# A pad and a moved table: the on-chip tensors of a split-fp32 transformer kernel shifted by 96 and 224 bytes

## The chip, the core and the metric

The kernel runs on one core of a Trainium2 chip. The metric is the device time of one execution in microseconds; before the change it is 969.88 us, the median of 3 runs (968.15 to 973.4).

## What is computed

Two transformer blocks, one after the other, on 256 tokens of width 1024, all in float32. The first mixes a windowed attention (8 heads, 2 key heads, with a sink logit) and a bidirectional chunkwise mLSTM, whose states come from 256 context tokens; its shifts, scales and gates come from a conditioning vector through `w_ada`. The second prepends 16 meta tokens (272 in all) and has two SwiGLU layers around a windowed attention with a gated linear attention. What fills the time are the dense products:

```
x = x + gt_m * rms_norm(concat(att, mlstm) @ w_out, g)
x = x + gt_f * rms_norm((silu(h @ Wg) * (h @ Wu)) @ w_ffn_out, g)            # width 2816
h = h + 0.5 * (silu(n @ ffn1_w_gate) * (n @ ffn1_w_up)) @ ffn1_w_down        # 272 tokens
h = h + (sigmoid(ga) * (ya @ w_branch_att) + sigmoid(gb) * (yb @ w_branch_gla)) @ w_out
out = rms_norm(h + 0.5 * swiglu(rms_norm(h), ffn2...), final)[:, 16:]        # 256 tokens
```

## The kernel before

**Layout of the work.** Activations lie transposed: 128 partitions by 8 tiles `k` of the model width, and the tokens (256, 258 or 272 columns) along the free dimension. A weight panel of 128 x 128 is the stationary operand, a token tile the moving one, and a product is written to a PSUM bank (`acc` or `wk`) of 512 columns.

**Split products.** Each float32 product is made of three fp32r products: the weights and the activations are each split into a rounded high part and the rest, and `split_mm` (L2003 to L2007) adds high x high (L2005), low activation x high weight (L2006) and high activation x low weight (L2007). L2398 (`mixed_part`), L2134 (`two_groups`) and L2203 to L2205 (`by_token`, where the weights are the moving operand) do the same in other orders.

**The rings.** Weights stream from HBM by SP's DMA queue into `raw`, four slots of 1408 floats per partition. For each slot ScalarE rounds `raw` to `hi` (L621), VectorE writes `lo = raw - hi` (L1143), and TensorE takes 24 matmuls from a slot of 1024 floats or 33 from one of 1408. ScalarE's split of slot j waits for TensorE's use of the slot's former content (`mm_done`), VectorE's for `hi_ready`, TensorE for `lo_ready`.

**The stages**, by the time of the profile: the first block's input projections with mLSTM and attention between them (to 190 us), `gu0` (gate and up of the first SwiGLU, 258 columns: the 256 tokens and two more, 190 to 320), `dn0` (its down product, 256 columns, 320 to 385), `gu1` and `dn1` (272 columns, 385 to 525 and 525 to 590), the second block's projections, attention and linear attention (590 to 740), `wout2` and `gu2` (256 columns, 740 to 890) and `dn2` (to the end). `n_high` and `n_low` hold the activations of `gu0`, `gu1` and the second mixer, `mixH` and `mixL` those of the output products and of `gu2`, `g_high` and `g_low` those of the down products, `n5H` and `n5L` the 512 tokens of the first projections.

**Where tensors lie.** `sbuf` (L117) takes on-chip tensors one behind the other from a stack; each begins at the next multiple of 32 bytes in the partition, and scopes that are closed give their space to later ones. The first one, `cst`, begins at byte 16512, a multiple of 64, and is 1544 bytes long, so what follows is shifted. Worked out from the declarations, the start of each in bytes, modulo 64 and 256:

| tensor | start | mod 64 | mod 256 |
|---|---|---|---|
| `cst` (identity, ones) | 16512 | 0 | 128 |
| `raw` | 33184 | 32 | 160 |
| `hi` / `lo` | 55712 / 78240 | 32 | 160 |
| `mixH` / `mixL` | 100960 / 109152 | 32 | 96 |
| `n5H` / `n5L` | 144928 / 161312 | 32 | 32 |
| `n_high` / `n_low` | 121888 / 132128 | 32 | 32 |
| `g_high` / `g_low` | 168032 / 192096 | 32 | 96 |
| `sg` | 216032 | 32 | 224 |
| `hbuf`, `row3` | 218240, 220416 | 0 | 128, 0 |
| `Sm` (first attention) | 183840 | 32 | 32 |
| `kdT`, `kS2`, `av2`, `gvtok`, `kdtok`, `St`, `attm`, `bias2`, `Sm2`, `pT2` | 192704 to 221440 | 0 | |

The steps inside a tensor are multiples of 64 bytes in all operands of the dense products: 128 weight columns are 512 bytes, a tile of 256 columns 1024, one of 272 columns 1088, the tiles of `mH` 1280 bytes apart, and the frames begin 16 columns (64 bytes) into a row. So all of these operands begin at 32 modulo 64.

Of the kernel before, what the change touches and what calls it, by code (L numbers as in the profile page):

```python
# [14 lines left out]
P = 128  # L15
# [99 lines left out]
def program(nc, dr, out):  # L115
    with ExitStack() as root:
        def sbuf(stack, name, shape, dt=F32):  # L117
            return stack.enter_context(nc.sbuf_tensor(name, shape, dt))
# [2 lines left out]
            return root.enter_context(nc.semaphore(name))  # L121


        cst = sbuf(root, "cst", [P, 3 * P + 2])
        ident, ones, swap, pick = cst[:, 0:P], cst[:, P:2 * P], cst[:, 2 * P:3 * P], cst[:, 3 * P:3 * P + 2]
        vec = sbuf(root, "vec", [P, NV])
# [4 lines left out]
        crow = sbuf(root, "crow", [P, D])  # L131
        R = sbuf(root, "R", [P, KD, TM])
        raw = sbuf(root, "raw", [P, RING, SLOT])
        slabs1 = ExitStack()
        slab_hi = sbuf(slabs1, "slab_hi", [P, RING, SLOT])
        slabs1.close()
        hi = sbuf(root, "hi", [P, RING, SLOT], F32R)
        lo = sbuf(root, "lo", [P, RING, SLOT], F32R)
        sinkn = sbuf(root, "sinkn", [P, 16])
        negm = sbuf(root, "negm", [P, 32])  # L140
        staged = ExitStack()
        stage = sbuf(staged, "stage", [P, 4, 1024])
        staged.close()
# [2655 lines left out]
```

## Time and profile before

| | |
|---|---|
| median of 3 runs | 969.88 us |
| span of the profiled execution | 969.3 us |
| TensorE busy | 954.7 us, 7543 matmuls |
| VectorE / ScalarE busy | 640.4 / 494.7 us |
| GpSimd busy | 68.8 us |
| read from HBM | 174.32 MB, 181 GB/s over the span |

The span runs from the first instruction to the last of one profiled execution. TensorE's matmuls overlap: a matmul's record lasts about 0.28 us while the next one begins after some 0.12 us, so the busy time does not tell how fast they run; what tells is the distance from one start to the next, or the number of matmuls in a stretch.

### The profile page before, as it was taken

Reading aid. Unit: us, or ns where it says so; the run is one execution under the profiler, and the core shown is the slowest. Engines: PE = TensorE matmul, PEld = TensorE weight load, DVE = VectorE, ACT = ScalarE, POOL = GpSimd, SP = SyncE. Lnnn points to the kernel's source line nnn. Section 1 sums busy time; section 2 is a strip of 40 time slices with the busy share of each in tenths; the row PEclk is TensorE's granted clock in tenths of the full one; section 3 lists DMA queues with packets and bytes.
Section 4 is the critical chain, followed back from the end, with each engine's and each line's share of the span. In section 5 each row is a group of like instructions: output and inputs, shape, how many; then the busy total and the mean of one; then the engine's idle time right before and its main releaser. Section 6 shows DMA issues by size and latency. Waiting matters only on the chain.

```text
span 969.3 us, 19405 instructions
## 1 busy us (share of the span) xinstructions
PE 954.7 (98%) x7543; PEld 886.8 (91%) x7543; DVE 640.4 (66%) x990; ACT 494.7 (51%) x762; POOL 68.8 (7%) x100
## 2 busy tenths in 40 slices
PE   8999999999999999999999999999999999999997
PEld 3776778899999999899999999999989999999997
DVE  4788887687666774765555546665778666565654
ACT  3755547664454543554444434645565555444540
POOL 0012002200000021000000000200210100000000
PEclk9999999999999999999999999999999999999999
DMA  9982437546566795276665944663445567567841
GB/s 348 384 282 89 131 131 237 181 165 201 180 187 184 203 299 164 63 215 174 173 174 169 238 114 137 212 185 88 132 134 173 167 181 209 179 182 220 215 119 43
DMA packets 189184, 176.06 MB, mean 182 GB/s; under 512 B 7313, under 2 KB 177825, under 8 KB 188753
## 3 DMA queue, kind: packets, MB, share of 16 engines
q1 hardware_dynamic: 183456, 154.29, 53.7%
q0 software_dynamic: 4960, 17.64, 5.2%
q10 hardware_dynamic: 720, 3.49, 0.9%
q8 instruction: 31, 0.51, 0.2%
q14 instruction: 17, 0.13, 0.1%
HBM read 174.32 MB, written 1.05 MB: 181 GB/s over the span
## 4 chain that ended last, share of the span: by engine, by line
PE 88%; DVE 6%; DMA 2%; ACT 2%; issue 1%; SPq 1%; POOL 0%; DVEq 0%; ACTq 0%
PE acc L2005 24%; PE acc L2006 24%; PE acc L2007 24%; PE acc L2398 2%; DMA slab_hi<-in_w_ada 1%; DMA stage<-in_w_late 1%; PE acc L2203 1%; PE acc L2205 1%; PE acc L2204 1%; PE wk L2005 1%; DVE lo L1143 1%; PE wk L2007 1%; PE wk L2006 1%; PE wk L2702 1%; PE wk L2134 1%
## 5 line engine op out<-in xcount | busy, mean ns | idle before, releaser
L1143 DVE TENSOR_TENSOR lo<-raw,hi 128x1024 fp32r<-128x1024 f32 (+1 forms) x259 | 331.6, 1291 | 211.4 <-ACT hi L621 211.1
L621 ACT ACTIVATE hi<-raw 128x1024 fp32r<-128x1024 f32 (+1 forms) x260 | 283.6, 1099 | 133.7 <-PE acc L2007 123.5
L2005 PE MATMUL acc<-n_high,hi 128*128 128x272 f32 (+3 forms) x1016 | 290.8, 286 | 0.3 <-DVE hbuf L1671 0.3
L2006 PE MATMUL acc<-n_low,hi 128*128 128x272 f32 (+3 forms) x1016 | 289.4, 285 | 0.0
L2007 PE MATMUL acc<-n_high,lo 128*128 128x272 f32 (+3 forms) x1016 | 288.4, 284 | 0.0
L2005 PEld LDWEIGHTS acc<-n_high,hi 128*128 128x128 f32 (+1 forms) x1016 | 191.6, 189 | 2.7 <-issue 1.4
L2006 PEld LDWEIGHTS acc<-n_low,hi 128*128 128x128 f32 (+1 forms) x1016 | 191.1, 188 | 0.5
L2007 PEld LDWEIGHTS acc<-n_high,lo 128*128 128x128 f32 (+1 forms) x1016 | 191.0, 188 | 0.2
L2006 PE MATMUL acc<-g_low,hi 128*128 128x256 f32 (+1 forms) x528 | 149.1, 282 | 0.0
L2005 PE MATMUL acc<-g_high,hi 128*128 128x256 f32 (+1 forms) x528 | 148.9, 282 | 0.0
L2007 PE MATMUL acc<-g_high,lo 128*128 128x256 f32 (+1 forms) x528 | 148.7, 282 | 0.0
L2005 PE MATMUL acc<-mixH,hi 128*128 128x256 f32 x400 | 113.0, 282 | 0.5 <-DVE gab L1844 0.4
L2006 PE MATMUL acc<-mixL,hi 128*128 128x256 f32 x400 | 112.3, 281 | 0.0
L2007 PE MATMUL acc<-mixH,lo 128*128 128x256 f32 x400 | 112.3, 281 | 0.0
L2006 PEld LDWEIGHTS acc<-g_low,hi 128*128 128x128 f32 x528 | 99.8, 189 | 0.0
L2005 PEld LDWEIGHTS acc<-g_high,hi 128*128 128x128 f32 x528 | 99.2, 188 | 0.2 <-issue 0.2
L2007 PEld LDWEIGHTS acc<-g_high,lo 128*128 128x128 f32 x528 | 99.2, 188 | 0.0
L2006 PEld LDWEIGHTS acc<-mixL,hi 128*128 128x128 f32 x400 | 76.6, 192 | 0.0
L2005 PEld LDWEIGHTS acc<-mixH,hi 128*128 128x128 f32 x400 | 75.1, 188 | 1.4 <-DVE gab L1844 0.7
L2007 PEld LDWEIGHTS acc<-mixH,lo 128*128 128x128 f32 x400 | 75.1, 188 | 0.0
L566 POOL TENSOR_TENSOR sq<-sq 128x256 f32<-128x256 f32 (+1 forms) x28 | 25.6, 915 | 479.9 <-ACT sq L923 431.9
L923 ACT ACTIVATE sq<-R (+3 forms) x36 | 15.9, 440 | 57.6 <-DVE R L1715 49.9
(424 smaller groups left out, 1246.6 us busy)
## 6 DMA issues: line engine op xcount, KB each, us to landing
raw<-in_w_in SPq DMA_DIRECT2D x52, 512.0 KB, 4.1
raw<-in_w_ffn_in SPq DMA_DIRECT2D x44, 512.0 KB, 3.8
raw<-in_ffn_w_gate SPq DMA_DIRECT2D x44, 512.0 KB, 3.9
raw<-in_ffn_w_up SPq DMA_DIRECT2D x44, 512.0 KB, 3.8
raw<-in_ffn_w_down SPq DMA_DIRECT2D x32, 704.0 KB, 4.8
stage<-in_w_late POOLq DMA_DIRECT2D x24, 512.0 KB, 5.1
raw<-in_w_ffn_out SPq DMA_DIRECT2D x16, 704.0 KB, 6.2
raw<-in_w_out SPq DMA_DIRECT2D x16, 512.0 KB, 4.4
```

The costliest lines, as they stand in the source:

```text
L566: ins = pool.tensor_tensor(sq[:, 0, 0:width], sq[:, 0, 0:width], sq[:, k, 0:width], ALU.add)
L621: act.activation(hi[:, j, 0:width], raw[:, j, 0:width], ACT.Copy).then_inc(hi_ready, 1)
L923: act.activation(sq[:, k, 0:width], R[:, k, t0:t0 + width], ACT.Square).then_inc(sq_ready, 1)
L1143: dve.tensor_tensor(lo[:, j, 0:width], raw[:, j, 0:width], hi[:, j, 0:width].bitcast(F32), ALU.subtract).then_inc(lo_ready, 1)
L2005: pe.matmul(out_, wH, xH, start=start, stop=False)
L2006: pe.matmul(out_, wH, xL, start=False, stop=False)
L2007: return pe.matmul(out_, wL, xH, start=False, stop=stop)
L2134: ins = pe.matmul(bank[:, T * m:T * m + T], ws[:, j, w], xs[:, k, 0:T], start=k == 0 and m == 0 and n == 0, stop=k == KD - 1 and n == 2, s ...
L2203: pe.matmul(out_, n5H[:, k, rows], hi[:, k // 2, w], start=k == 0, stop=False)
L2204: pe.matmul(out_, n5H[:, k, rows], lo[:, k // 2, w], start=False, stop=False)
L2205: return pe.matmul(out_, n5L[:, k, rows], hi[:, k // 2, w], start=False, stop=k == KD - 1)
L2398: ins = pe.matmul(out_, ws[:, j, w], xs[:, k, :], start=k == 0 and m == 0 and n == 0, stop=k == KD - 1 and n == 2, skip_group_check=True)
```

## The change

A tensor of 24 floats (96 bytes) that nothing uses is declared ahead of `cst`, and `negm`, a table of 32 floats (128 bytes), is declared between `raw` and `slab_hi`/`hi` in place of behind `sinkn`. No instruction, no wait and no order is changed.

```diff
+        sbuf(root, "pad_0", [P, 24])
         cst = sbuf(root, "cst", [P, 3 * P + 2])
...
         raw = sbuf(root, "raw", [P, RING, SLOT])
+        negm = sbuf(root, "negm", [P, 32])
         slabs1 = ExitStack()
...
         sinkn = sbuf(root, "sinkn", [P, 16])
-        negm = sbuf(root, "negm", [P, 32])
```

By the same working, everything moves by 96 bytes, and what lies between `raw` and `sinkn` (`slab_hi`, `hi`, `lo`, `sinkn`) by 224:

| tensor | start after | mod 64 | mod 256 |
|---|---|---|---|
| `cst` | 16608 | 32 | 224 |
| `raw` | 33280 | 0 | 0 |
| `hi` / `lo` | 55936 / 78464 | 0 | 128 |
| `mixH` / `mixL` | 101056 / 109248 | 0 | 192 |
| `n5H` / `n5L` | 145024 / 161408 | 0 | 128 |
| `n_high` / `n_low` | 121984 / 132224 | 0 | 128 |
| `g_high` / `g_low` | 168128 / 192192 | 0 | 192 |
| `sg` | 216128 | 0 | 64 |
| `hbuf`, `row3` | 218336, 220512 | 32 | 224, 96 |
| `kdT` to `pT2` | 192800 to 221536 | 32 | |

The last tensor ends at byte 229312.

## Rows read from the trace of the kernel before

**Rows 1.** The page: TensorE's share, its granted clock by slice, the chain that ended last

```profile
PE 954.7 (98%) x7543; PEld 886.8 (91%) x7543; DVE 640.4 (66%) x990; ACT 494.7 (51%) x762; POOL 68.8 (7%) x100
...
PEclk9999999999999999999999999999999999999999
...
PE 88%; DVE 6%; DMA 2%; ACT 2%; issue 1%; SPq 1%; POOL 0%; DVEq 0%; ACTq 0%
```

**Rows 2.** Busy time by stretch: us, each engine with its instructions, clock, DMA, GB/s

```profile
20.00:60.00 40.00, 38.20 (x240) 29.60 (x240) 32.76 (x71) 25.91 (x46) 3.91 (x10) 1.00 0.96 345
...
340.00:370.00 30.00, 30.00 (x267) 30.00 (x267) 21.36 (x22) 13.24 (x16) 8.00 (x8) 1.00 0.99 280
470.00:500.00 30.00, 30.00 (x242) 30.00 (x241) 17.67 (x19) 13.62 (x18) 0.00 (x0) 1.00 0.59 173
250.00:280.00 30.00, 30.00 (x251) 30.00 (x250) 19.36 (x28) 15.85 (x23) 0.00 (x0) 1.00 0.58 177
790.00:820.00 30.00, 30.00 (x258) 30.00 (x256) 19.64 (x21) 16.30 (x22) 0.00 (x0) 1.00 0.71 210
```

**Rows 3.** TensorE in order of time, 735 us: start us, duration us, instruction

```profile
734.98 0.28 PE L2005 MATMUL acc<-mixH,hi 128*128 128x256 f32 x1
...
735.89 0.28 PE L2007 MATMUL acc<-mixH,lo 128*128 128x256 f32 x1
```

**Rows 4.** The same view at 738 us, behind a piece of attention

```profile
736.77 1.02 PE L2702 MATMUL wk<-pT,av 16*64 16x128 f32 x12
...
738.21 0.28 PE L2007 MATMUL acc<-mixH,lo 128*128 128x256 f32 x1
...
738.92 0.28 PE L2007 MATMUL acc<-mixH,lo 128*128 128x256 f32 x1
```

**Rows 5.** Groups by shape: line, engine, instruction, shapes, count, busy us, mean ns, idle

```profile
L2006 PE MATMUL acc<-n_low,hi 128*128 128x272 f32 x400 | 115.7, 289 | 0.0
...
L2006 PE MATMUL acc<-mixL,hi 128*128 128x256 f32 x400 | 112.3, 281 | 0.0
...
L2006 PE MATMUL acc<-g_low,hi 128*128 128x256 f32 x352 | 98.0, 279 | 0.0
L2006 PE MATMUL acc<-n_low,hi 128*128 128x258 f32 x336 | 95.8, 285 | 0.0
...
L2006 PE MATMUL acc<-n_low,hi 128*128 128x256 f32 x272 | 75.6, 278 | 0.0
...
L2006 PE MATMUL acc<-g_low,hi 128*128 128x272 f32 x176 | 51.0, 290 | 0.0
```

**Rows 6.** TensorE in order of time: 512 columns, weights of 16 columns

```profile
68.41 0.40 PE L2006 MATMUL wk<-n5L,hi 128*16 128x512 f32 x1
...
69.33 0.40 PE L2007 MATMUL wk<-n5H,lo 128*16 128x512 f32 x1
```

**Rows 7.** The same: 512 columns, weights of 128 columns

```profile
109.60 0.39 PE L2204 MATMUL acc<-lo,n5H 128*128 128x512 f32 x1
...
110.52 0.40 PE L2205 MATMUL acc<-hi,n5L 128*128 128x512 f32 x1
```

**Rows 8.** The same: four plain fp32 matmuls of 256 columns, merged

```profile
63.37 1.02 PE L2183 MATMUL wk<-qT,c 128*128 128x256 f32 x4
```

**Rows 9.** Groups by shape: one operation on tensors at 0 and at 32 modulo 64

```profile
L1691 DVE TENSOR_TENSOR hbuf<-acc,inv 128x512 f32<-128x512 f32 x11 | 7.5, 681 | 0.0
...
L944 ACT ACTIVATE sg<-sg 128x512 f32<-128x512 f32 x11 | 7.0, 632 | 21.0 <-DVE sg L1663 21.0
...
L1685 DVE TENSOR_TENSOR sg<-acc,inv 128x512 f32<-128x512 f32 x10 | 6.8, 681 | 0.0
...
L948 ACT ACTIVATE g_high<-hbuf 128x512 f32 x9 | 5.7, 632 | 18.2 <-DVE hbuf L1671 18.2
```

**Rows 10.** Who waited for whom: us in total, times, longest

```profile
DVE lo L1143 <- ACT hi L621: 211.1, 178, 3.9
...
ACT hi L621 <- PE acc L2007: 123.5, 84, 4.2
```

## The prediction

> **What bounds the kernel now.** [...] Then the busy times by stretch: from about 190 us on, TensorE has work in every microsecond of a stretch, while VectorE is busy 15 to 21 us of 30 and the DMA engines move 173 to 280 GB/s [rows 2]. Last the waits: ScalarE's splits wait for TensorE to free a slot, VectorE's for ScalarE, so the ring is full and the matmuls set the pace [rows 10]. The time is the number of matmuls times the distance between their starts, and the change can only act on that distance, on the other engines' durations, or on the DMAs.
>
> [...] A stretch of 30 us sees every matmul whose record (0.28 us) touches it, so the distance is 30.28 us over the count [rows 2]: 113 ns in `dn0` (256 columns, 267 matmuls), 117 ns in `gu2` (256 columns, 258), 121 ns in `gu0` (258 columns, 251), 125 ns in `gu1` (272 columns, 242). [...] Single starts give the same with more digits: (735.89 - 734.98) / 8 = 114 ns in one streak of 256 columns [rows 3], (738.92 - 738.21) / 6 = 118 ns in the next one, behind twelve small attention matmuls [rows 4]. So there are two paces with the same tensors at the same addresses, the fast and the slow one. DMA traffic doesn't choose: the fast pace holds at a DMA share of 0.99, the slow one at 0.71 [rows 2].
>
> [...]
>
> **The change part by part.** No instruction is added, removed or moved, so each queue, SP's and GpSimd's too, issues the same in the same order; the pad and the moved table cost nothing by themselves.
>
> VectorE and ScalarE: `hbuf` begins at 0 and `sg` at 32 modulo 64, and the same operation takes 681 ns on either, ScalarE's 632 ns reading either [rows 9]. Nothing, in both directions.
>
> Dense matmuls, counts from the groups, each standing for three lines [rows 5]: 272 columns (400 + 176) x 3 = 1728; 258 columns 336 x 3 = 1008; 256 columns (400 + 352 + 272) x 3 = 3072. With those on other lines or banks I take 1780, 1060 and 3450. Some 1250 of the 256-column ones run at the fast pace (`dn0`, `w_out`, most of the second projections), 2150 at the slow one (all of `gu2` and `dn2`, part of the first projections). [...]
> - 256 columns, slow: 2150 x 6.7 = 14.4 us.
> - 256 columns, fast: the floor seems to be the columns plus about 2 ns, so 113.3 - 109 = 4.2 ns, x 1250 = 5.3 us.
> - 272 columns: 1780 x 6.7 = 11.9 us.
> [...]
> - 512 columns: some 290 x 6.7 = 2.0 us.
>
> The sum is 33.6 us. What hides it: before 190 us part of the matmuls wait beside attention, mLSTM and the start-up loads, so I let 95% through, 32 us. In the dense stages the next bound is far: 30 us of `dn0` hold 21.4 us of VectorE, of `gu2` 19.6 us, and a TensorE 4 to 6% faster keeps below that [rows 2]. `dn0` is the one place where the DMA engines are at 0.99 [rows 2]; should they bind there, some 3 us of the gain stay out.
>
> [...]
>
> DMAs: the rows written to `raw` begin at 0 instead of 160 modulo 256. Where that could count is the start-up, 20 to 60 us at a DMA share of 0.96 and 345 GB/s [rows 2], but the later stages have spare bandwidth. No row prices it; between -3 and +1 us, and I take 0.
>
> The small operands go the other way: `cst` and the second block's attention tensors leave 0 modulo 64 for 32. [...]
>
> [...]
>
> **The rivals.**
> [...]
> (b) Slower: the two paces are a pattern between the reads of weights and moving operand, started by what ran before [rows 3, 4]. The change moves `hi` and `lo` by 128 bytes against everything else modulo 256. If that is what chooses the pattern, the slow pace takes the fast stretches, 1250 x 4.4 = 5.5 us, 272 columns go from 125 to about 130 ns (1780 x 5 = 8.9 us) and 258 from 121 to 126 (5.3 us): 20 us, 990 us. [...] For: the slow pace exists. Against: modulo 128 the distance is kept.
> [...]
> [...]
>
> **How the numbers follow.** The profiled span of 969.3 us stands 0.6 us below the median of the runs, so the sum is made against 969.9: 969.9 - 32 = 938 us. Chances: forecast (930 to 947) 0.41; (c) 0.12; (d) 0.09; (a) 0.18; (b) 0.20. Faster by over 0.5% (under 965 us) is 0.62, within 0.5% (about what a measurement of this kernel can tell from no change) 0.18, slower 0.20. The range must keep (a) and half of (b) and most of (d): 918 to 982. The likeliest case alone would be 928 to 948.
>
> **What would show it.** Counts in 30 us of a steady stretch: `gu2` from 258 to about 273, `gu1` from 242 to about 255, `gu0` unchanged at 251. [...] If `dn0` falls to 258, (b). VectorE's and ScalarE's means must stay at 681 and 632 ns. The prediction is wrong if the path doesn't care for 64 bytes, which nothing in this trace can exclude.

## The result, and the profile after

The changed kernel takes 973.38 us (median, 971.48 to 975.48), the kernel before, run beside it, 970.01 us (968.03 to 973.4): a ratio of 1.0038, 95% interval 1.0023 to 1.0053. The forecast was 938 us. It is 0.4% slower, not 3% faster; no part of the expected gain came. The measured time lies in the range of 918 to 982 us only because the range was stretched to hold the rivals.

The page after has nearly the same TensorE time as [rows 1], 955.3 us against 954.7, and 9 in every slice of the clock, as before. The profiled execution is the quickest of the eight of the changed kernel (971.48 us).

```profile
span 969.7 us, 19405 instructions
...
PE 955.3 (99%) x7543; PEld 888.5 (92%) x7543; DVE 639.9 (66%) x990; ACT 494.6 (51%) x762; POOL 68.2 (7%) x100
...
PEclk9999999999999999999999999999999999999999
...
PE 88%; DVE 6%; ACT 2%; issue 1%; DMA 1%; SPq 1%; DVEq 0%; ACTq 0%
```

Busy time by stretch of the kernel after, columns and stretches as in [rows 2], and one stretch more, in `dn2`, where the kernel before has 257 matmuls, too:

```profile
20.00:60.00 40.00, 38.81 (x246) 30.46 (x246) 33.68 (x74) 26.46 (x47) 4.39 (x11) 1.00 0.95 352
...
340.00:370.00 30.00, 30.00 (x267) 30.00 (x266) 20.86 (x21) 13.23 (x16) 7.79 (x6) 1.00 0.91 281
470.00:500.00 30.00, 30.00 (x242) 30.00 (x242) 17.67 (x20) 13.62 (x18) 0.00 (x0) 1.00 0.60 170
250.00:280.00 30.00, 30.00 (x251) 30.00 (x250) 20.11 (x28) 15.15 (x22) 0.00 (x0) 1.00 0.59 176
790.00:820.00 30.00, 30.00 (x257) 30.00 (x256) 19.46 (x20) 16.52 (x22) 0.00 (x0) 1.00 0.69 210
905.00:935.00 30.00, 30.00 (x257) 30.00 (x256) 15.96 (x16) 12.10 (x12) 2.23 (x3) 1.00 0.80 234
```

From 190 us on each count is that of before to within one matmul: 267 in `dn0` (256 columns), 242 in `gu1` (272), 251 in `gu0` (258), 257 for 258 in `gu2` (256). Had the forecast's 6.7 ns a matmul come, `gu1` would show 255 and `gu2` 273. The other engines didn't move either: the operations of [rows 9] in the kernel after, groups by shape, the same columns, are 681 and 632 ns again.

```profile
L1692 DVE TENSOR_TENSOR hbuf<-acc,inv 128x512 f32<-128x512 f32 x11 | 7.5, 681 | 0.0
...
L945 ACT ACTIVATE sg<-sg 128x512 f32<-128x512 f32 x11 | 7.0, 632 | 21.1 <-DVE sg L1664 21.1
```

To see where 0.4% went I took the distances between starts stage by stage, leaving out gaps over 150 ns. Two stages of 256 columns show it: `w_out` (192 matmuls) goes from 114.3 to 117.8 ns, the second block's projections (816) from 115.2 to 116.8. `dn0` stays at 113.5, `gu2` and `dn2` at 117.7. Windows in which TensorE alone is listed (us, busy, count, clock, DMA share, GB/s), before:

```profile
163.00:178.00 15.00, 14.99 (x128) 1.00 0.70 219
...
690.00:720.00 30.00, 30.00 (x265) 1.00 0.44 135
```

and after:

```profile
163.00:178.00 15.00, 15.00 (x124) 1.00 0.62 206
...
690.00:720.00 30.00, 30.00 (x261) 1.00 0.44 134
```

`w_out` falls from 128 to 124 in 15 us, 3%. In all, 1247 of the 3456 starts of 256 columns were at most 116 ns apart before, 709 after: 538 x 4.5 ns = 2.4 us more. Some 264 matmuls of 512 columns became 3 ns shorter, 0.8 us less. That makes 1.6 us, for a difference of 3.4 us between the medians and 0.4 us between the two profiled spans (969.7 and 969.3). Part of the rest is a gain that works the other way: the start-up became quicker. TensorE has 246 matmuls from 20 to 60 us where it had 240, and reaches its 600th matmul at 111.2 us instead of 112.5.

### The profile page after: what moved, and what is told of

Same layout as the page of the kernel before. It is cut to its first block, busy times and chain, and to the rows that moved or that the text cites. A ratio compares the mean times of both kernels' runs of the same rounds, so it can differ in the third digit from the quotient of the medians.

```text
span 969.7 us, 19405 instructions
## 1 busy us (share of the span) xinstructions
PE 955.3 (99%) x7543; PEld 888.5 (92%) x7543; DVE 639.9 (66%) x990; ACT 494.6 (51%) x762; POOL 68.2 (7%) x100
## 4 chain that ended last, share of the span: by engine, by line
PE 88%; DVE 6%; ACT 2%; issue 1%; DMA 1%; SPq 1%; DVEq 0%; ACTq 0%
PE acc L2006 24%; PE acc L2007 24%; PE acc L2008 24%; PE acc L2399 2%; DMA slab_hi<-in_w_ada 1%; PE acc L2204 1%; PE acc L2206 1%; PE acc L2205 1%; PE acc L2135 1%; PE wk L2006 1%; PE wk L2008 1%; PE wk L2007 1%; DVE lo L1144 1%; PE wk L2703 1%; PE wk L2135 1%
```

## The experiments

Two questions: does the start modulo 64 matter at all, and what chooses between the two paces? The change does two things that can be made one at a time: the pad moves the operands of the dense products to multiples of 64 and keeps all distances; the table `negm` ahead of `hi` moves `slab_hi`, `hi`, `lo` and `sinkn` by 128 bytes against all other tensors, and so the weights against the moving operands. In what follows, distance means the start of the weights less the start of the moving operand, modulo 512 bytes. The steps between the weights used in `hi` and `lo` are multiples of 512 (but for the few products with 16 columns of weights), and so are those between the tiles of `mixH` and of `g_high` at 256 columns. The distance is 320 there in the kernel before and 448 in the kernel after. The tiles of `mH`, from which the 256-column frames of the second block's projections are read, are 1280 bytes apart: there the distance alternates between this value and one 256 bytes away, 64 and 320 before, 192 and 448 after.

The kernels of one group of experiments ran on one chip, beside the kernel before, and each is compared with the median of before on that chip.

**The pad alone** (`e_pad`):

```diff
+        sbuf(root, "pad_0", [P, 24])
         cst = sbuf(root, "cst", [P, 3 * P + 2])
```

> The pad of 96 bytes alone: everything moves by 96 bytes, the distance of hi and lo from the others is that of before. Theory A (addresses don't matter to the matmuls; the pace of 256 columns, 113.3 or 117.8 ns, is picked anew wherever TensorE starts again from a wait): between 968 and 975 us, with the stretches at 117.8 ns distributed anew, no rule in it. Theory C (the distance of the weights from the moving operands modulo 256 picks the pace): 970.0 us, the stretches of w_out and of the second projections at 113.3 ns as before.

967.62 us for 968.99, ratio 0.9985 (0.9974 to 0.9996). All big operands begin at 0 modulo 64, and `gu1` stays at 242, `gu0` at 251, `gu2` at 257. Nothing of the forecast's 6.7 ns a matmul is there. The time is just under what either theory said.

```profile
250.00:280.00 30.00, 30.00 (x251) 30.00 (x250) 20.11 (x28) 15.16 (x22) 0.00 (x0) 1.00 0.60 182
340.00:370.00 30.00, 30.00 (x257) 30.00 (x256) 19.73 (x20) 12.94 (x16) 7.41 (x6) 1.00 0.84 264
470.00:500.00 30.00, 30.00 (x242) 30.00 (x242) 17.58 (x18) 13.69 (x19) 0.00 (x0) 1.00 0.60 175
```

In this execution `dn0` runs at the slow pace (257) with the distance it had before. It is the slowest of the kernel's 11 executions (971.78 us, 4.2 above their median), so what it shows need not be what the others did. The start-up is quicker here, too: the 600th matmul begins at 111.1 us, in the kernel after at 111.2 and in its repetition at 111.3, against 111.8 to 112.5 in the nine profiled executions without the pad of 96 bytes. That is 1.2 us between the medians, most of the 1.37 us by which this kernel is faster than before.

**The table alone** (`e_negm`), starts staying at 32 modulo 64:

```diff
+        negm = sbuf(root, "negm", [P, 32])
         slabs1 = ExitStack()
         ...
         sinkn = sbuf(root, "sinkn", [P, 16])
-        negm = sbuf(root, "negm", [P, 32])
```

> The moved table alone: hi, lo and slab_hi move by 128 bytes, everything else stays, all at 32 modulo 64. Theory A: between 968 and 975 us, no rule in which stretches run at 117.8 ns. Theory C: 973.4 us as after the whole change, with w_out and the second projections at 117.8 ns.

973.95 us for 968.99, 1.0054 (1.0039 to 1.0069). It is at least the whole cost of the change: the moved table is what makes the kernel slower, the pad is not. The two parts add up: 4.96 us more and 1.37 us less are 3.6 us, and the whole change costs 3.4. The forecast of the distance theory was 973.4 us with `w_out` and the second projections at 117.8 ns, and they run at 117.7 and 117.6.

Its profiled execution holds something else: the granted clock falls to half (0.50) for 6.8 us in the first block. The stretch around it, in which TensorE alone is listed (us, busy, count, clock, DMA share, GB/s), and then the same in the kernel before:

```profile
155.70:162.50 6.80, 6.80 (x31) 0.50 0.98 357
```

```profile
155.70:162.50 6.80, 6.47 (x50) 1.00 0.94 336
```

From the 700th matmul to the 1100th the kernel before takes 54.0 us and this one 56.8, so the fall costs it 2.8 us. In the 5 us ahead of it TensorE did about the same in both (36 matmuls in 150 to 155 us before, 39 here), so these rows don't tell why it came. The profiled executions of `e_d0` and `e_all128` have a fall of 3.4 us at about the same place.

**A pad of 64 bytes** (`e_pad64`), which keeps starts modulo 64 and distances, as a control:

```diff
+        sbuf(root, "pad_0", [P, 16])
         cst = sbuf(root, "cst", [P, 3 * P + 2])
```

> A pad of 64 bytes, table in its old place: every tensor keeps its place modulo 64 and its distance from the others. Theory A: 968 to 975 us. [...]

The distance theory has 970.0 us here, too, with the same stretches at 113.3 ns as before. It took 968.23 us for 968.99, 1.0005 (0.9993 to 1.0016): nothing. Yet `dn2` runs at the fast pace in its profiled execution and at the slow one in that of the kernel before, with the same distances and starts modulo 64.

**A kernel of matmuls only** (`m1`) runs sections of 48 matmuls from tensors that are complete beforehand, each with other starts of the moving operand (`mo`) and the weights (`wo`). It computes nothing of the reference. Its loop, cut, where `term` goes through the three split products and `k` counts from 0 to 7:

```python
W = (wa, wa, wb)[term]; X = (xa, xb, xa)[term]
w = slice(wo + P * (k % 7), wo + P * (k % 7) + P)
x = slice(mo + 512 * (k % 7), mo + 512 * (k % 7) + width)
...
ins = pe.matmul(o, W[:, w], X[:, x], start=True, stop=True)
```

In theory A, the surplus is what a matmul takes beyond its columns' own time, and a full-rate stream is one of fp32r matmuls.

> A kernel of its own that computes nothing of the reference: sections of 48 fp32r matmuls on an otherwise idle core, with the operands of the three split terms in turn, moving and stationary operands begun 0, 4, 8, 16, 32, 48 bytes behind a multiple of 64, widths of 192 to 512 columns, and variants (same operands throughout, one high part, one weight, four banks, 16 weight columns, plain fp32). Theory A (the surplus belongs to the full-rate stream, whatever the start): 256 columns at 113 or 118 ns from every start, 272 at 125, 512 at 227 to 232, plain fp32 at 213 to 216 ns. [...]

TensorE in order of time in `m1` (start us, duration us, instruction). Each pair of lines is 20 starts apart; the sections stand in the order both at 0; moving operand 32 bytes on; weights 64 bytes on; both 32 bytes on:

```profile
22.27 0.28 PE L110 MATMUL acc<-xa,wb 128*128 128x256 f32 x1
...
24.67 0.28 PE L110 MATMUL acc<-xb,wa 128*128 128x256 f32 x1
...
47.42 0.28 PE L110 MATMUL acc<-xa,wa 128*128 128x256 f32 x1
...
49.76 0.28 PE L110 MATMUL acc<-xa,wb 128*128 128x256 f32 x1
...
90.76 0.28 PE L110 MATMUL acc<-xb,wa 128*128 128x256 f32 x1
...
93.03 0.28 PE L110 MATMUL acc<-xa,wa 128*128 128x256 f32 x1
...
97.08 0.28 PE L110 MATMUL acc<-xa,wa 128*128 128x256 f32 x1
...
99.48 0.28 PE L110 MATMUL acc<-xa,wb 128*128 128x256 f32 x1
```

2.40 / 20 = 120 ns, 2.34 / 20 = 117, 2.27 / 20 = 113.5, 2.40 / 20 = 120 again. Over whole sections the values are 120.0, 116.7, 113.3 and 120.0. Moving both operands by 32 bytes changes nothing (120.0), moving one does (116.7 or 118.3): what counts is the distance, not the start. With the weights 64 and the moving operand 32 bytes on, a distance of 32, it is 118.3, as with the weights alone 32 bytes on. Theory A, with 113 or 118 ns from every start, didn't have this. And a moving operand that begins at 0 modulo 64 is here the slower one, by 3 ns, where the forecast had it the faster by 7.

The same kernel tells what the surplus is made of. At distance 0, 256, 384 and 512 columns take 120.0, 173.3 and 226.7 ns, so 128 columns more cost 53.3 and 53.4 ns: 0.417 ns a column, or 106.7 ns for 256. That is an estimate from these three widths at one distance; it leaves 256 columns a surplus of 13.3 ns there. Weights of 16 columns instead of 128 bring 256 columns at distance 0 from 120.0 to 113.3 ns; with the moving operand 32 bytes on (distance 480) it is 116.7 with either. So the weights' width counts at one distance and not at another. The same weights, the same operand or four banks in turn leave it at 120.0 at distance 0. 192 columns take 111.7 ns, only 8.3 less than 256, where the estimate gives their columns 80 ns, so at this width something other than the columns sets the pace. A plain fp32 matmul of 256 columns stands as two records, 96 for the 48 of its section, and each takes 215.8 ns at either start.

**A kernel over all distances** (`m2`), in steps of 32 bytes; the loop is that of `m1` with `k % 6` for the weights, and it computes nothing of the reference, either. Cut:

```diff
-        for wo in (1, 4, 8, 16):
-            section(256, 0, wo)
...
+        for w in (256, 272, 258, 512):
+            for i in range(16):
+                section(w, 0, 8 * i, "one", n=33)
+        for i in range(16):
+            section(256, 0, 8 * i, "split", n=33)
...
```

> The kernel of its own again (nothing of the reference is computed): sections of 33 fp32r matmuls, the moving operand at 0 and the stationary one at 0, 32, 64 ... 480 bytes behind it modulo 512, for 256, 272, 258 and 512 columns, then the three split terms at 256 columns, then moving rows of 1088 bytes one behind the other as in gu1 and gu0, then 256 columns with one to five small matmuls ahead. Theory C (the distance of the weights from the moving operand picks the pace), as the first such kernel suggests: 256 columns at 120.0 ns at distance 0, 118.3 at 32, 113.3 at 64, 116.7 at 96. If only the distance modulo 128 counts, 192 bytes gives 113.3 ns as 64 does, and the loss of the change isn't explained; if modulo 256 counts, 192 (the distance of the output products after the change) is slower than 64 (that of before) or has both paces by what runs ahead. Theory A: no pattern by distance.

TensorE in `m2` in order of time, each line one section of 33 matmuls, distances 32, 64 and so on to 256 in order:

```profile
24.63 4.16 PE L109 MATMUL acc<-xa,wa 128*128 128x256 f32 x33 [0.25 <-DVE tiny L68]
29.05 4.03 PE L109 MATMUL acc<-xa,wa 128*128 128x256 f32 x33 [0.25 <-DVE tiny L68]
33.33 4.18 PE L109 MATMUL acc<-xa,wa 128*128 128x256 f32 x33 [0.25 <-DVE tiny L68]
37.76 4.18 PE L109 MATMUL acc<-xa,wa 128*128 128x256 f32 x33 [0.25 <-DVE tiny L68]
42.19 4.22 PE L109 MATMUL acc<-xa,wa 128*128 128x256 f32 x33 [0.25 <-DVE tiny L68]
46.67 4.01 PE L109 MATMUL acc<-xa,wa 128*128 128x256 f32 x33 [0.25 <-DVE tiny L68]
50.93 4.12 PE L109 MATMUL acc<-xa,wa 128*128 128x256 f32 x33 [0.25 <-DVE tiny L68]
55.30 4.20 PE L109 MATMUL acc<-xa,wa 128*128 128x256 f32 x33 [0.25 <-DVE tiny L68]
```

64 and 192 are the short ones (4.03 and 4.01 us). In ns between starts, the first dozen of a section left out, 256 columns, once with one pair of operands ("one") and once with the three terms that the kernel uses ("terms"):

| distance | one | terms | | distance | one | terms |
|---|---|---|---|---|---|---|
| 0 | 120.0 | 120.0 | | 256 | 120.0 | 120.0 |
| 32 | 118.2 | 118.3 | | 288 | 118.2 | 118.3 |
| 64 | 113.3 | 117.8 | | 320 | 113.3 | 117.8 |
| 96 | 118.7 | 117.4 | | 352 | 117.4 | 118.7 |
| 128 | 118.7 | 118.7 | | 384 | 118.7 | 118.7 |
| 160 | 119.9 | 120.1 | | 416 | 119.9 | 120.1 |
| 192 | 113.3 | 117.8 | | 448 | 117.8 | 117.8 |
| 224 | 116.7 | 116.7 | | 480 | 116.7 | 117.9 |

Three groups: about 120 at 0 and 256, 118.7 at 128 and 384, and at 64, 192 and 320 either 113.3 or 117.8. These two are the kernel's fast and slow pace. In further sections small matmuls (n of them of 64n columns, n from 1 to 5) ran ahead of the same stream. At distance 64 they gave 117.8, 113.3, 113.3, 113.3, 117.8; at 192 117.8, 113.3, 117.8, 113.3, 117.8; at 448 117.8 each time, 7 of 7 with the two of the table; at 128 120.2 once and then 118.7. The theory's guess of 116.7 ns at 96 missed (118.7 and 117.4). The table repeats itself after 256 bytes, as far as one distance has one value at all: the pair that differs most is 192 (3 of 7 fast) and 448 (none of 7), and the whole kernel has these two the other way about. The first two of them at distance 64, TensorE in order of time in `m2`, again 20 starts between the two lines of each stream:

```profile
511.58 0.30 PE L79 MATMUL wk<-xa,wa 128*128 128x64 f32 x1 [0.25 <-DVE tiny L68]
...
513.09 0.28 PE L109 MATMUL acc<-xa,wb 128*128 128x256 f32 x1
...
515.45 0.28 PE L109 MATMUL acc<-xb,wa 128*128 128x256 f32 x1
...
516.10 0.44 PE L79 MATMUL wk<-xa,wa 128*128 128x128 f32 x2 [0.25 <-DVE tiny L68]
...
517.68 0.28 PE L109 MATMUL acc<-xa,wb 128*128 128x256 f32 x1
...
519.95 0.28 PE L109 MATMUL acc<-xb,wa 128*128 128x256 f32 x1
```

2.36 / 20 = 118 ns behind one kind of start, 2.27 / 20 = 113.5 behind the other, with the same tensors: what ran just before sets which pace a stream keeps.

Other widths in `m2`: 512 columns take 226.7 ns at 0 and 256, 229.0 at 192 and 448, 232.5 at 128 and 384, 233.3 to 234.4 elsewhere. 258 and 272 columns from rows of 1088 bytes, as the kernel has them, take 119.6 to 120.7 and 124.8 to 126.3 at every distance; such rows, 64 bytes on modulo 512 from one to the next, pass through many distances. `gu0`, `gu1` and `dn1` have them and stayed where they were in every kernel (120.8, 125.1, 125.9 to 126.1). From tiles 2048 bytes apart the same widths do answer, 119.0 to 122.2 and 123.3 to 126.7.

**The distance kept, `hi` moved by 128 bytes** (`e_all128`): if only the place of `hi` against `raw` and the small tensors mattered, this would cost what `e_negm` costs.

```diff
+        sbuf(root, "pad_0", [P, 32])
         slabs1 = ExitStack()
```

> A pad of 128 bytes between raw and hi, the table in its old place: hi, lo, the mixer's, the projections' and the SwiGLU's operands all move by 128 bytes together; only raw, the residual and what is ahead of them stay. Theory C (weights against moving operands): the time of before, 969 us, with the second projections mostly at 113.3 ns. If instead the place of hi itself, or its distance from raw (which ScalarE and VectorE read), made the moved table slow: 974 us.

966.01 us for 970.91, 0.9950 (0.9931 to 0.9969): not slower but faster, and 3 us under the 969 us of the distance theory. Since all operands behind `raw` moved together, this keeps the distance and changes the place of `hi`; the moved table of `e_negm` is slow by the distance and not by that place. The stretches in `gu2` and `dn2`, columns as in [rows 2], show 266 matmuls for 258 and 267 for 257, the fast pace:

```profile
790.00:820.00 30.00, 30.00 (x266) 29.99 (x266) 20.83 (x22) 16.25 (x22) 0.00 (x0) 1.00 0.73 216
905.00:935.00 30.00, 30.00 (x267) 30.00 (x266) 16.79 (x19) 12.52 (x12) 2.22 (x3) 1.00 0.75 205
```

**Four other distances in the whole kernel.** The table of `m2` now made forecasts. Edits, all in the order of the tensors (the tables' lines at their old places go, and are not shown):

```diff
 # e_d0: distance 0
+        sinkn = sbuf(root, "sinkn", [P, 16])
+        negm = sbuf(root, "negm", [P, 32])
         slabs1 = ExitStack()
 # e_d384: distance 384
+        sinkn = sbuf(root, "sinkn", [P, 16])
         slabs1 = ExitStack()
 # e_d64: distance 64, negm ahead of hi and mods behind lo
-        mods = sbuf(root, "mods", [P, 48, 2])
+        negm = sbuf(root, "negm", [P, 32])
         slabs1 = ExitStack()
         ...
+        mods = sbuf(root, "mods", [P, 48, 2])
 # e_d192: distance 192
         negm = sbuf(root, "negm", [P, 32])
+        sbuf(root, "pad_0", [P, 32])
```

> Both small tables (sinkn, 64 bytes, and negm, 128) ahead of hi: hi and lo move by 192 bytes, so that the weights lie 0 modulo 512 from mixH, g_high and the frames, in place of 320 (before) and 448 (after the change). Theory C2 (the pace of 256 columns is a function of that distance modulo 512, as the second kernel of its own measured it): all 256-column stretches at 120.0 ns, 512 columns at 227 in place of 232; 3000 matmuls lose 2.3 ns against 117.8: 978 to 983 us. Theory A (chance): 964 to 975 us with 113 and 118 ns stretches.

> Only sinkn ahead of hi: distance 384. Theory C2: 256 columns at 118.7 ns throughout, 974 to 978 us. Theory A: 964 to 975 us with 113 and 118 ns stretches.

> negm ahead of hi and mods (384 bytes) behind lo: distance 64. Theory C2: both 113.3 and 117.8 ns, by stretch, as at 320: 964 to 972 us, no stretch at 120 or 118.7. Theory A: the same, so this run alone doesn't tell them apart; it shows whether 64 is better than 320.

> A pad of 128 bytes behind negm: hi, lo and raw stay, the moving operands of the output products, down products and second mixer move by 128: distance 192. Theory C2: 113.3 and 117.8 ns by stretch as at 320, 964 to 972 us.

Against 973.23 us for before on the same chip: `e_d0` 982.13 us, 1.0089 (1.0072 to 1.0106); `e_d384` 979.16 us, 1.0070 (1.0053 to 1.0087); `e_d64` 970.23 us, 0.9973 (0.9960 to 0.9985); `e_d192` 975.85 us, 1.0025 (1.0014 to 1.0036). `dn0`, `gu2` and `dn2` of `e_d0`, columns as in [rows 2]:

```profile
340.00:370.00 30.00, 30.00 (x253) 30.00 (x252) 21.02 (x23) 13.15 (x16) 6.65 (x8) 1.00 0.98 282
...
790.00:820.00 30.00, 30.00 (x251) 29.98 (x251) 19.95 (x20) 16.37 (x23) 0.00 (x0) 1.00 0.64 187
905.00:935.00 30.00, 30.00 (x253) 30.00 (x251) 17.15 (x15) 14.57 (x14) 0.75 (x1) 1.00 0.78 207
```

and of `e_d384`:

```profile
340.00:370.00 30.00, 30.00 (x255) 30.00 (x254) 21.20 (x21) 12.04 (x16) 6.90 (x8) 1.00 0.97 277
...
790.00:820.00 30.00, 30.00 (x255) 30.00 (x254) 20.02 (x21) 16.04 (x22) 0.00 (x0) 1.00 0.68 193
905.00:935.00 30.00, 30.00 (x255) 30.00 (x254) 18.64 (x18) 15.26 (x15) 1.48 (x2) 1.00 0.82 215
```

30.28 / 253 = 120 ns and 30.28 / 255 = 119 ns, against 113 and 117 in the kernel before: both values of `m2` are there, in every stage of 256 columns. Averaged over all starts it is 119.8 to 120.0 in all five stages of `e_d0` and 118.7 to 118.8 in those of `e_d384`. The forecasts of 978 to 983 and 974 to 978 us met 982.13 and 979.16. `e_d64` came out in its range of 964 to 972 us, with both paces. The forecast for `e_d0` also said 227 ns for 512 columns; that is the value at 0, but `n5H` is then at 64 (and at 448 where it is the weights), and the trace has 233.1 and 229.5 ns, as `m2` at 64 and 448. In `e_d192` I had expected the fast pace now and then, 964 to 972 us, and it missed: all five stages are at the slow pace, 117.4 to 117.8.

**The two that mattered, once more** (`all128_again`, `after_again`; the edits are those above), since a pace that is drawn may be drawn another way on another chip or execution.

> The pad of 128 bytes between raw and hi once more, on another chip, beside the kernel before and the changed one. Theory C2 leaves the pace at distance 320 to what runs ahead of a stretch: if that is fixed by the program, gu2 and dn2 are at 113.3 ns again and the time is 0.4 to 0.6% under the kernel before; if it is drawn anew in each execution, the times spread over 963 to 973 us and the mean is that of before.

> The changed kernel once more. Theory C2: distance 448, gu2 and dn2 at 117.8 ns again, 0.3 to 0.5% over the kernel before. Should gu2 come out at 113.3 ns here, the distance of 448 doesn't hold it slow in the whole kernel as it did in seven starts of seven in the second kernel of its own.

Against 971.33 us (23 runs of before on that chip, 970.22 to 973.57): `after_again` 974.06 us, 1.0020 (1.0008 to 1.0031); `all128_again` 970.28 us, 0.9985 (0.9965 to 1.0005), with 12 runs from 963.72 to 975.31 us. The changed kernel is slower a second time, by less than the forecast's 0.3 to 0.5%, with `gu2` and `dn2` at 117.8 ns as foreseen. The granted clock isn't the reason: the executions with a mean of 0.998 or more have a median of 974.04 us (7) against 971.11 (11 of before). The other one isn't faster for certain: its executions spread over 1.2%, those of before over 0.3%. Its profiled execution was a quick one, 961.9 us, with `gu2` at the fast pace:

```profile
790.00:820.00 30.00, 30.00 (x267) 29.99 (x266) 20.56 (x21) 15.69 (x22) 0.00 (x0) 1.00 0.73 222
```

The stages of 256 columns side by side, ns between starts, one profiled execution of each kernel:

| kernel | distance | `w_out` | `dn0` | projections 2 | branches to `gu2` | `dn2` |
|---|---|---|---|---|---|---|
| matmuls | | 192 | 528 | 816 | 1248 | 528 |
| before | 320 | 114.3 | 113.4 | 115.2 | 117.6 | 117.8 |
| `e_pad` | 320 | 116.2 | 117.6 | 114.3 | 117.6 | 117.8 |
| `e_pad64` | 320 | 113.9 | 113.4 | 114.0 | 117.0 | 113.6 |
| `e_all128` | 320 | 114.0 | 113.4 | 114.2 | 114.0 | 113.4 |
| `all128_again` | 320 | 113.7 | 113.4 | 114.0 | 113.7 | 113.4 |
| `e_d64` | 64 | 113.9 | 113.4 | 114.1 | 117.0 | 117.8 |
| after | 448 | 117.8 | 113.6 | 116.8 | 117.7 | 117.8 |
| `after_again` | 448 | 117.2 | 113.6 | 117.5 | 117.8 | 117.8 |
| `e_negm` | 448 | 117.7 | 113.6 | 117.6 | 117.6 | 113.6 |
| `e_d192` | 192 | 117.7 | 117.8 | 117.4 | 117.6 | 117.8 |
| `e_d384` | 384 | 118.7 | 118.7 | 118.8 | 118.7 | 118.7 |
| `e_d0` | 0 | 119.8 | 120.0 | 119.8 | 120.0 | 120.0 |

At 320 and 64 one to five of the five stages are fast, at 448 one or two, at 192 none; at 384 and 0 all stages have one pace of their own. With the frames alternating by 256 bytes, what fits all kernels is the distance modulo 256: 64 (before) is mostly fast, 192 (after) mostly slow, 128 gives 118.7 and 0 gives 120.0. The times agree: the four results at 448 and 192 lie 0.2 to 0.5% over before, the five at 320 and 64 between 0.5% under and the same. One profiled execution can't show it, since `e_pad` at 320 has fewer fast starts (839) than `e_negm` at 448 (1061).

The paces do account for the profiled spans. The distances between the starts of the dense matmuls, gaps over 150 ns left out (280 ns at 512 columns), add up to 792.8 us in the kernel before, 794.0 after, 784.0 in `all128_again` and 803.5 in `e_d0`, and in each of the twelve executions the rest of the span is 175 to 179 us.

## Why the prediction was wrong, point by point

**What bounds the kernel, and by what formula.** This held. From 784.0 to 803.5 us of settled starts the span followed, within the 4 us by which the rest varies. A sum of the prediction's kind gives for `e_d0` 1247 x (120.0 - 113.5) + 2209 x (120.0 - 117.8) = 13 us more; counted start by start it is 10.7, since 192 matmuls of 272 columns from the tiles of `mH` went from 126.6 to 123.4 ns and those of 256 columns on `n5H` from 118.6 to 115.6. The two profiled spans differ by 11.6 us, the medians by 8.9.

**What the matmuls lose to.** I had taken the weights to be without effect and the loss to be the moving operand's alone, and this is the step that failed first. I had it from 512 columns, which take 230 ns, (69.33 - 68.41) / 4, with weights of 16 columns [rows 6] and 230 ns, (110.52 - 109.60) / 4, with weights of 128 [rows 7]. At 256 columns the weights do count: 113.3 ns with 16, 120.0 with 128 at distance 0 in `m1`, though not at 480 (116.7 with either). At 512 columns they count at distance 0 too, the other way about: 231.6 ns with 16, 226.7 with 128, at distance 0. The two groups of rows aren't even at the same distance (from 384 on in steps of 64 bytes with 16 columns of weights, and 128 where `hi` is the moving operand and `n5H` the weights), and the distance moves 512 columns by up to 7.7 ns in `m2`; that they agree was no proof about the load. The surplus is partly a matter of the two operands' places against each other, which is the thing the change altered and I had put aside.

**6.7 ns a matmul.** The sum of the forecast takes 6.7 ns off each matmul of 256 (slow), 272 and 512 columns, and 4.2 ns off the fast ones of 256, down to a floor of 109 ns. No run shows either number as the worth of a start at 0 modulo 64, and they weren't worked out from the rows: they were my guess. What the runs show in their place is 120.0 ns in `m1` with both operands at 0 and with both at 32, and the fast pace with operands at 0 modulo 64 (113.3 ns in `m1` with the weights 64 bytes on) as well as with operands at 32 (113.4 in `dn0` of the kernel before). The case in which the prediction ends by calling itself wrong, a path for the operands that doesn't care for 64 bytes, is the one that came. For the 6.7 ns I had that 17 such steps come to about 113.3 ns, the fast pace. The rows on hand already spoke against it: in steps of 6.7 ns from 113.3 the widths had to take 113.3, 120.0 or 126.7 ns, and 226.7 or 233.3 ns, and 258 columns took 121, 272 columns 125, 512 columns 230. A number that a theory hits exactly was one number: in the trace all operands of the dense products begin at 32 modulo 64, and yet the forecast got 0.41. The terms built on it (14.4, 5.3, 11.9 and 2.0 us) didn't come, 33.6 us in all: `e_pad` changes just this, keeps the counts of `gu0`, `gu1` and `gu2` and gives -0.15%, most of which its quicker start-up accounts for.

**VectorE, ScalarE, plain fp32.** As forecast, nothing. 681 and 632 ns stand as they were, and the records of plain fp32 matmuls begin 215.8 ns apart at both starts in `m1`. What I read from [rows 8] was wrong, though. With 0.38 us for the last record, the four are (1.02 - 0.38) / 3 = 213 ns apart, and I took each for a matmul. They are two matmuls (the loop at that line issues two, and `m1` has two records for each), so a plain fp32 matmul of 256 columns takes twice 213 ns. In `m1` it is twice 215.8 ns, where the fp32r kind takes 120.0 and 116.7 ns at the same two starts.

**DMAs.** I put the start-up at 0, between -3 and +1 us. It came 1.2 us quicker in the three profiled executions with the pad of 96 bytes, in which the DMA engines moved 351 to 355 GB/s from 20 to 60 us, against 345 to 350 in the nine without it. That it is the new start of `raw` rather than of another tensor was not tested.

**The rivals.** (a), nothing at all, 970 us, is what the start modulo 64 does to the dense matmuls. (c) and (d) were gains of another size, to 955 and to 914 to 922 us, and nothing of them came. (b) is what the change does: the table's move changes the distance and the slow pace takes fast stretches. Its mechanism was right, its size was not, 20 us for 3.4. Two of its terms hardly exist: 272 and 258 columns in rows of 1088 bytes don't answer to the distance (8.9 and 5.3 us). The third, 5.5 us for all 1250 fast matmuls, became 2.4 us in the profiled execution, since only `w_out` and part of the projections turned slow and `dn0` did not; the sign it gave to `dn0` (a fall to 258) was wrong in both executions of it that were profiled (113.6 ns in each). My argument against (b), that modulo 128 the distance is kept, was wrong: in `m2` 320 was fast once in two and 448 never in seven, and 0 and 128 differ by 1.3 ns. In the whole kernel `dn0` is fast at 448 as well, so the difference is one of how often. The 512-column matmuls gained as `m2` says, TensorE in order of time in the kernel after, five starts between the lines:

```profile
109.50 0.39 PE L2204 MATMUL acc<-hi,n5H 128*128 128x512 f32 x1
...
110.63 0.39 PE L2206 MATMUL acc<-hi,n5L 128*128 128x512 f32 x1
```

1.13 / 5 = 226 ns, against 230 in [rows 7]: their distance went from 128 to 0, where `m2` has 226.7.

**Other starts.** Moved by 32 bytes together, the operands of `m1` keep their 120.0 ns: of the start alone, 0 or 32 modulo 64 is the same there, and I weighed this case too lightly. A moving operand that starts 4 or 8 bytes on is dear in `m1`, 123.4 and 126.7 ns, against 118.7 at 16; weights that start 4 bytes on are not, 118.4 ns as at 16. Each of these starts has its own distance as well, so the two effects aren't separated.

**What stays open.** Why 256 columns never take less than 113.3 ns. What exactly ahead of a stream chooses 113.3 or 117.8, why `dn0` is fast at 448 where `m2` was slow 7 times of 7, and why nothing is fast at 192 in the whole kernel where `m2` was fast 3 times of 7. Then the size of the slowdown. In the profiled execution of the kernel after, the paces cost 1.2 to 1.6 us and the start-up gains 1.2, which fits the 0.4 us between the spans; but this execution is 1.9 us quicker than its median. In that of `e_negm` the paces add nothing (its `dn2` is fast) and the fall of the clock costs 2.8 us, which covers the 2.3 us between the spans; but its five executions, at mean clocks from 0.995 to 0.999, all take 972.7 us or more. So the median of the slowdown rests on executions without a profile. That more of their stages run at the slow pace is likely and wasn't shown. The two profiled executions of the kernel after have nearly the same stages fast, and so have the two of the pad of 128 bytes, so how far a pace is drawn anew in each execution stays open, too.

## What to carry to other kernels

Where a stream of matmuls sets the time, the place of the weights against the moving operand counts, modulo 256 bytes as far as these runs tell, and their common start modulo 64 does not: from 113.3 to 120.0 ns for 256 columns here. So read the addresses before you move a table or put in a pad, keep the distance, and measure it with a kernel of matmuls alone ahead of any forecast from sizes. Where a pace may be drawn anew, one profile is one draw: compare its time with the median before you explain the median by it. A theory that hits one number exactly has still been tested once: put it to the other widths in the same rows, look for a second start in the trace, and if there is none, let the chance say so.

## What the runs showed of the hardware that I had not expected

- The same stream with the same addresses has two lasting paces, 113.3 and 117.8 ns, by what ran just before it, at distances 64, 192 and 320 in `m2`.
- The order over distances isn't the same for all widths: distance 0 is among the slowest for 256 columns (120.0 ns, against 113.3 at the best) and the fastest for 512 (226.7, against 234.4 at the worst).
- At distance 0, 192 columns take 111.7 ns, nearly as long as 256 at their fast pace.
- A moving operand that starts 4 or 8 bytes on takes 3.4 or 6.7 ns more than the 120.0 at 0; weights that start 4 bytes on take 1.6 ns less.
- The executions of one kernel can spread over 1.2% (`all128_again`, 963.72 to 975.31 us). Part of it is the granted clock: `e_d192` takes 974.68 to 975.22 us at a mean of 0.998 and 977.51 at 0.994. Part is not: four executions of `all128_again` at 0.998 take 963.72, 964.78, 965.77 and 972.28 us. Some 3400 matmuls of 256 columns at 4.5 ns between the paces would allow 15 us, an estimate; which pace the slower ones drew wasn't profiled.
- The pad of 96 bytes brought the 600th matmul 1.2 us forward.
